# A hybrid DeltaNet and RG-LRU layer: the opening stage reordered, shift and scale of the modulation made as columns, the gate third made in the last scan

## What is computed

```python
xs = x_sample + grid_pos_embed(...)             # sin/cos of 16 grid rows (512 wide) and 64 columns (512 wide)
mod = silu(c) @ ada_w + ada_b                   # once with c_ctx (context), once with c (latent): 3 x 1024
shift, scale, gate = split(mod, 3)
h = rmsnorm(x, pre_w) * (1 + scale) + shift
proj = h @ w_in                                 # q, k, v, z, beta/decay, rg input, rg gate
o_dn = delta_branch(...)                        # 8 heads of 128, both directions, chunks, decays, conv, gated norm
o_rg = rglru_branch(...)                        # width 1024 in 8 blocks, both directions
y = concat([o_dn, o_rg]) @ w_out
return x + gate * rmsnorm(y, post_w), states
```

## Time and profile before

| what | us |
|---|---|
| median of 3 runs | 1523.67 (1518.97 to 1530.37) |
| the profiled execution | 1524.72 |
| its span | 1523.1 |
| PE busy in it | 1391.1 (91%) |
| DVE, ACT, POOL busy | 1027.9, 753.3, 115.3 |

### The profile page before, as it was taken

The page is one execution under the profiler, slowest core; times in us unless marked ns, Lnnn a source line. Parts: engine busy times, 40 slices in busy tenths (PEclk is TensorE's granted clock), DMA queues, the critical chain, the costliest instruction groups (busy, mean ns, idle before and its releaser), DMA issues.

```text
span 1523.1 us, 24595 instructions
## 1 busy us (share of the span) xinstructions
PE 1391.1 (91%) x8182; PEld 1248.2 (82%) x8182; DVE 1027.9 (67%) x2135; ACT 753.3 (49%) x1912; POOL 115.3 (8%) x135
## 2 busy tenths in 40 slices
PE   5966899999999989999999999899989997599997
PEld 1266898899799879988997998799889976388886
DVE  3565477779677877887797778778877966722222
ACT  2351357564646465565647464745666484511111
POOL 0000100010001000100000010001000000212211
PEclk9978999999799999999999999999999998699999
DMA  8702111110111211111111111102111150523440
GB/s 306 249 14 68 28 29 32 57 44 30 40 49 44 57 48 28 60 33 42 44 44 36 53 44 49 55 22 67 33 42 45 44 225 20 153 77 110 124 123 29
DMA packets 95235, 102.79 MB, mean 67 GB/s; under 512 B 4230, under 2 KB 81271, under 8 KB 94089
## 3 DMA queue, kind: packets, MB, share of 16 engines
q1 hardware_dynamic: 92170, 90.70, 19.4%
q0 software_dynamic: 2944, 10.49, 1.8%
HBM read 85.88 MB, written 15.29 MB: 66 GB/s over the span
## 4 chain that ended last, share of the span: by engine, by line
PE 77%; ACT 8%; DVE 6%; issue 5%; DMA 3%; SPq 0%; DVEq 0%; ACTq 0%
PE bank L673 14%; PE bank L675 14%; PE bank L674 14%; PE bank L947 12%; PE bank L901 2%; PE bank L868 2%; PE bank L784 2%; PE bank L909 2%; PE bank L917 2%; PE bank L894 2%; PE bank L889 2%; PE bank L824 2%; DMA arena<-pos_row 2%; PE bank L746 1%; ACT L1089 1%
## 5 line engine op out<-in xcount | busy, mean ns | idle before, releaser
L673 PE MATMUL bank<-hT_hi,w_hi 128*128 128x384 f32 (+1 forms) x1224 | 442.0, 361 | 30.9 <-DVE w_lo L1379 17.6
L675 PE MATMUL bank<-hT_hi,w_lo 128*128 128x384 f32 (+1 forms) x1224 | 419.4, 343 | 0.0
L674 PE MATMUL bank<-hT_lo,w_hi 128*128 128x384 f32 (+1 forms) x1224 | 419.4, 343 | 0.0
L673 PEld LDWEIGHTS bank<-hT_hi,w_hi 128*128 128x128 f32 x1224 | 235.8, 193 | 33.7 <-DVE w_lo L1379 18.5
L674 PEld LDWEIGHTS bank<-hT_lo,w_hi 128*128 128x128 f32 x1224 | 235.9, 193 | 1.2
L675 PEld LDWEIGHTS bank<-hT_hi,w_lo 128*128 128x128 f32 x1224 | 234.9, 192 | 0.0
L1225 ACT ACTIVATE arena<-bank,arena 128x128 f32<-128x128 f32 x272 | 78.7, 369 | 176.2 <-PE bank L901 176.0
L1469 DVE SCALAR_TENSOR_TENSOR arena<-arena 128x1154 f32<-128x1154 f32 x96 | 137.5, 1433 | 3.5 <-DVE arena L1467 1.1
L947 PE MATMUL bank<-wo_hi,ot_hi 128*128 128x512 f32 x288 | 114.3, 397 | 18.8 <-DVE ot_lo L1758 13.5
L947 PE MATMUL bank<-wo_lo,ot_hi 128*128 128x512 f32 x288 | 113.6, 395 | 0.0
L947 PE MATMUL bank<-wo_hi,ot_lo 128*128 128x512 f32 x288 | 113.3, 393 | 0.0
(11 more groups left out here) (224 smaller groups left out, 2388.4 us busy)
## 6 DMA issues: line engine op xcount, KB each, us to landing
w_raw<-w_in SPq DMA_DIRECT2D x51, 512.0 KB, 4.0
arena<-ada_w SPq DMA_DIRECT2D x8, 1536.0 KB, 10.8
arena<-scr_G SPq DMA_DIRECT2D x16, 576.0 KB, 4.8
ot<-scr_o SPq DMA_DIRECT2D x9, 1024.0 KB, 6.7
arena<-x_sample SPq DMA_DIRECT2D x16, 512.0 KB, 7.3
wo<-w_out SPq DMA_DIRECT2D x4, 2048.0 KB, 16.0
scr_o<-arena POOLq DMA_DIRECT2D x8, 576.0 KB, 4.2
arena<-pos_row SPq DMA_DIRECT2D x32, 128.0 KB, 5.5
```

The source lines that it names most:

```text
L673: pe.matmul(out, w_hi[:, slot, k], hT_hi[:, k, cols], start=first, stop=False)
L674: pe.matmul(out, w_hi[:, slot, k], hT_lo[:, k, cols], start=False, stop=False)
L675: return pe.matmul(out, w_lo[:, slot, k], hT_hi[:, k, cols], start=False, stop=last)
```

## The change

- ada_w is loaded in the opening for shift and scale alone (eight slabs of 1 MB). Its product is made as columns: 128 columns of ada_w are the weights, the two columns of silu_c move, 16 products for each of eight k, all in bank 0, which one product with zeros opens. Biases come as columns too. The six row sums and the 16 turns are gone.
- All nine tiles of x have a buffer, and SP issues all loads of the opening without a wait between them. The row half of the position comes from PE (a selection matrix times the 16 rows, into banks 1 and 2), the column half is added by POOL. DVE, ACT and PE work on different tiles in one round i: DVE adds the position row to tile i, makes the mean of i - 1, reciprocal and scale of i - 2, and copies tile i - 3; ACT squares i, takes the root of i - 1 and copies i - 3. The copies to hT are one instruction of 512 columns each.
- Modulation, high and low parts go by column group and k, and PE waits for each k of a group. The order of products is ba(0), k(0), ba(1), ba(2), k(1), transposes, k(2). In DVE's stream the three convolutions move up before and between the sums; ACT's high_w, take_first and Silu are placed anew.
- The gate third: SP loads 4 MB of ada_w, silu_c (by way of DRAM) and the bias before w_out; the last scan waits for them and has 16 products of 512 columns, two in a step; DVE adds the bias after mean_o, SP stores the rows. No wait for gate_stored is left in the opening.
- POOL clears only the border columns of raw.

```diff
-SEGMENTS = [(0, 0, P), (1, P + GAP, 2 * P), (1, P + GAP + 2 * P, 3 * P), (1, P + GAP + 5 * P, 3 * P)]
+SEGMENTS = [[(0, 0, P), (1, P + GAP, 2 * P)], [(1, P + GAP + 2 * P, 3 * P)], [(1, P + GAP + 5 * P, 3 * P)]]
...
-        adaw = early(KT * 3 * D).rearrange("p (k n) -> p k n", k=KT)
-        x_in = early(2 * D).rearrange("p (b n) -> p b n", b=2)
+        adaw = early(KT * 2 * D).rearrange("p (k n) -> p k n", k=KT)
+        x_in = early(NCH * D).rearrange("p (b n) -> p b n", b=NCH)
+        pos_row_in, pos_col_in, row_pick = early(D // 2)[0:16, :], early(D // 2), early(D)[0:16, :]
...
+            for t in range(1, NCH):
+                sp.dma_start(x_in[:, t], x_sample[0, P * (t - 1):P * t, :]).then_inc(x_loaded[t], 16)
+            for k in range(6):
+                load_ada(k)
+            load_w(1, w_in2[:, OFF_B:OFF_B + P].rearrange("(k p) n -> p k n", p=P))
+            load_ada(6)
+            load_ada(7)
+            load_w(0, w_tile("k", 0))
...
+            sp.wait_ge(silu_c_made, 1)
+            sp.dma_start(scr_c, silu_c.rearrange("p s k -> p (s k)")).then_inc(silu_c_stored, 16)
@@ SP, before the w_out loads @@
             sp.wait_ge(projected.sem, projected.prev(h, 18))
+            sp.wait_ge(proj_taken.sem, proj_taken.prev(h, 12))
+            sp.wait_ge(silu_c_stored, 16)
+            sp.dma_start(silu_c_late.rearrange("p s k -> p (s k)"), scr_c).then_inc(gate_in, 16)
+            sp.dma_start(gate_row, ada_b[0:1, 2 * D:].to_broadcast([2, D])).then_inc(gate_in, 16)
+            for q in range(2):
+                sp.dma_start(adaw_gate[:, 4 * q:4 * q + 4, :],
+                             ada_w[0, 512 * q:512 * q + 512, 2 * D:].rearrange("(k p) n -> p k n", p=P)).then_inc(gate_in, 16)
...
+            sp.wait_ge(gate_row_made, 2)
+            sp.dma_start(scr_gate, gate_row).then_inc(gate_stored, 16)
@@ POOL @@
+            gp.wait_ge(pos_in, 48)
+            for n in range(1, NCH):
+                gp.wait_ge(x_loaded[n], 16)
+                gp.tensor_tensor(x_in[:, n, 512:], x_in[:, n, 512:], pos_col_in, ALU.add).then_inc(pos_col_added, 1)
             gp.wait_ge(x_turned, 2 * NCH)
-            gp.memset(raw, 0.0).then_inc(raw_cleared, 1)
             own(gp.memset(sub[0], 0.0))
-            gp.wait_ge(mod_row_made, 6)
-            gp.wait_ge(mod_turned, 1)
-            gp.wait_ge(gate_stored, 16)
             gp.memset(Z, 0.0).then_inc(grounds_made, 1)
+            gp.wait_ge(ada_done, 1)
+            gp.memset(raw[:, :, 0:2], 0.0).then_inc(raw_cleared, 1)
+            gp.memset(raw[:, :, RAW - 1:], 0.0).then_inc(raw_cleared, 1)
@@ PE @@
+            def put_pos_row(n):
+                if n >= 3:
+                    pe.wait_ge(x_added, n - 2)
+                pe.matmul(banks[1 + n % 2][:, :], row_pick[:, P * (n - 1):P * n], pos_row_in, start=True, stop=True)\
+                  .then_inc(pos_row_put, 1)
+            def ada_columns(k):
+                pe.wait_ge(ada_in[k], 16)
+                if k == 0:
+                    pe.matmul(banks[0][:, 0:32], ident, zeros, start=True, stop=False)
+                for m in range(16):
+                    mm = pe.matmul(banks[0][:, 2 * m:2 * m + 2], adaw[:, k, P * m:P * m + P], silu_c[:, :, k],
+                                   start=False, stop=(k == KT - 1 and m == 15))
+                if k == KT - 1:
+                    mm.then_inc(ada_done, 1)
+            put_pos_row(1)
+            for i in range(1, NCH + 2):
+                if i + 1 < NCH:
+                    put_pos_row(i + 1)
+                if i >= 2:
+                    turn_x(i - 2)
+                if i >= 5:
+                    ada_columns(i - 5)
+            for k in range(NCH - 3, KT):
+                ada_columns(k)
...
-            for g, (o, n) in enumerate(GROUPS):
-                pe.wait_ge(h_lo_made, KT * (2 + g) + 1)
-                ...
-            project_first(0)
+            pe.wait_ge(w_lo_made.sem, 1)
+            project_ba(0)
+            pe.wait_ge(w_lo_made.sem, 2)
+            project_k(0)
+            project_ba(1)
+            project_ba(2)
+            project_k(1)
             pe.wait_ge(baT_made, 3)
...
+            project_k(2)
             project_first(1)
@@ PE, last scan: gate_product(k, half) is one matmul 128*2 x 128x512 into bank half @@
                 pe.wait_ge(dZ_taken.sem, dZ_taken.at(b, 30))
+                if last:
+                    pe.wait_ge(gate_in, 16 * 4)
+                    pe.wait_ge(gate_tanh.sem, gate_tanh.at(b, 12))
...
                         fill(1)
+                        if last:
+                            gate_product(step - 1, 0)
...
                     fill(1)
+                    if last and step:
+                        gate_product(step - 1, 1)
...
+            pe.wait_ge(gate_row_made, 2)
             out_tile(0, 0, first=True)
@@ ACT, opening @@
+            for i in range(NCH + 3):
...
+            high_w(1, 16)
+            for g in range(len(GROUPS)):
+                for k in range(KT):
+                    high_h(g, k)
+                    if k + MOD_V < KT:
+                        modulate(g, k + MOD_V)
+                if g == 0:
+                    high_w(0, 16)
-            for n in range(3):
-                take_first(n)
+            take_first(0)
+            take_first(1)
+            high_w(1, 32)
...
-            high_w(1, 32)
-            for n in range(3, 6):
-                take_first(n)
+            take_first(2)
+            take_first(3)
+            high_w(0, 32)
+            take_first(4)
+            take_first(5)
...
-            high_w(0, 32)
-            act.wait_ge(gate_stored, 16)
             act.wait_ge(conv_done.sem, 1)
+            act.activation(kT, RA, ACT.Silu, scale=2.0).then_inc(silued.sem, 1)
             high_w(1, 48)
+            take_first(6)
             act.wait_ge(conv_done.sem, 2)
+            act.activation(qT, RB, ACT.Silu, scale=2.0).then_inc(silued.sem, 1)
+            take_first(7)
+            take_first(8)
+            high_w(0, 48)
@@ DVE @@
+            for i in range(NCH + 3):
...
+            low_w(1, 1)
+            dve.wait_ge(ada_done, 1)
...
+            for g in range(len(GROUPS)):
+                for k in range(MOD_V - 2):
+                    modulate(g, k)
+                for k in range(KT):
+                    low_h(g, k)
+                    if k < 2:
+                        modulate(g, MOD_V - 2 + k)
+                if g == 0:
+                    low_w(0, 2)
...
+            conv_first(0, RA)
+            low_w(0, 4)
             dve.wait_ge(G_summed, 3)
...
+            conv_first(1, RB)
+            low_w(1, 5)
             dve.wait_ge(grounds_made, 1)
             dve.wait_ge(G_stored, 32)
             dve.wait_ge(cols_ready, 1)
+            conv_first(2, xf)
+            low_w(0, 6)
...
             mean_o(HEADS - 1)
+            for half in range(2):
+                dve.wait_ge(gate_done, half + 1)
+                cc = slice(512 * half, 512 * half + 512)
+                dve.tensor_tensor(gate_row[:, cc], gate_row[:, cc], banks[half][0:2, :], ALU.add).then_inc(gate_row_made, 1)
             norm_o(HEADS - 1)
```

More of the change, by code:

```diff
@@ L655, in _ @@
                     mm.then_inc(x_turned, 1)
-                if n < KT:
-                    pe.wait_ge(ada_in[n], 16)
-                    for j in range(6):
-                        mm = pe.matmul(banks[j][0:2, :], silu_c[:, :, n], adaw[:, n, 512 * j:512 * j + 512],
-                                       start=(n == 0), stop=(n == KT - 1))
-                        if n == KT - 1:
-                            mm.then_inc(ada_done, 1)
-            pe.wait_ge(h_made_v, 4 * NCH)
-            for m in range(16):
-                pe.wait_ge(mod_row_made, m // 4 + 1)
-                mm = pe.transpose(banks[6][:, 2 * m:2 * m + 2], mod_row[0:2, P * m:P * m + P], ident[0:2, 0:2])
@@ L1335, in _ @@
                 own(dve.tensor_scalar(to, to, -1.0, None, ALU.mult))
-            def x_tile(buf, n, loaded):
-                prompt = isinstance(n, int) and n == 0
-                dve.wait_ge(x_loaded[buf], loaded)
-                if not prompt:
-                    dve.tensor_tensor(x_in[:, buf], x_in[:, buf], pos[:, buf], ALU.add).then_inc(x_added, 1)
-                dve.wait_ge(x_squared, n + 1)
-                dve.tensor_scalar(x_ss[:, buf:buf + 1], x_ss[:, buf:buf + 1], 1.0 / D, EPS, ALU.mult, ALU.add)\
-                   .then_inc(x_meaned, 1)
-                dve.wait_ge(x_rooted, n + 1)
-                own(dve.reciprocal(x_ss[:, buf:buf + 1], x_ss[:, buf:buf + 1]))
-                dve.tensor_scalar(x_in[:, buf], x_in[:, buf], x_ss[:, buf:buf + 1], None, ALU.mult).then_inc(x_normed, 1)
-                dve.wait_ge(x_turned, 2 * n + 1)
-                first = 0 if prompt else GAP + P * n
-                for k in range(4):
-                    dve.tensor_copy(hT[:, k, bd(first, P)], banks[6][:, P * k:P * k + P]).then_inc(h_made_v, 1)
@@ L1380, in low_w @@
                    .then_inc(w_lo_made.sem, 1)
```

(28 more changed lines are left out.)

270 lines of the change are left out of this document (121 added, 149 removed).

## The result

The changed kernel takes 1571.3 us (median of 4 runs, 1561.1 to 1584.2) against 1523.2 for the kernel before; the ratio is 1.0315 with a 95% interval of 1.0228 to 1.0402. The profiled execution took 1568.78 us with a span of 1567.1, 44.0 more than the span before.

A forecast was written before the change was run, and what follows sets the result against it. PE was taken as the bound, busy 91% of the span. From 1524.7 us, 14.2 less until the modulation, 33.8 less to the first head and 8 more in the last scan gave 1484.7, stated as 1485; range 1468 to 1512.

The forecast's parts named there:

- The head loop is not touched: Head loop: PE nearly dense there and code unedited, so the forecast gave it no term.
- A: Opening until the modulation: it starts at 63 in place of 77.17, 14 us earlier; bounds 49 and 98.
- rival 2: Opening: clock low from start to end, modulation at 98, 35 us more, 1520, no difference; chance 0.08.
- the 0.10 us a pass: Opening's column products on PE: 256 passes at 0.10 us, 3.25 us a k, eight k 26 us.
- rival 3: Opening's column passes, slower case: no overlap with the next weight load, up to 0.34 us a pass, 1546; chance 0.04.
- B: From modulation to first head: turn(kT) 73.5 us after the modulation, 33.8 us less; bounds 36 and 22.
- C: Last scan with the gate's 16 products: 8 us more; bounds 0 and 21.
- the 2.7 us taken off: Last scan: about 1.7 us back where ACT's Silu pair holds PE, about 1 from fewer steps at the lower clock.

The follow-up runs named there:

- run 1: Changed kernel with 72 satisfied waits (36 instructions) more at the start of PE's stream, ahead of the head loop; 1529.87 us, ratio 1.0021.
- run 2: Kernel before with 132 satisfied waits (66 instructions) more, putting its loop where the changed kernel has it; 1563.18 us, ratio 1.0266.
- run 10: Kernel of run 9 with 198 satisfied waits (99 instructions) at the start, putting the loop back at the changed kernel's place; 1529.97 us, ratio 1.0012.
- run 5: Kernel of run 1 with 32 moving columns in the ada products, silu_c's two and 30 of zeros; 1524.43 us, ratio 0.9983.
- Run 6: Changed kernel with shift and scale made as rows again (512 columns of ada_w moving) and one pair of transpose banks; 1498.33 us, ratio 0.9799.
- Run 4: Kernel of run 1 without 12 of the 16 gate products in the last scan; 1528.45 us, ratio 1.0002.
- run 9: Kernel of Run 6 with five idle products of 320 columns in each joins, where PE stands; 1488.04 us, ratio 0.9733.
- run 11: Kernel before with the five idle products in each joins and nothing of the change; 1518.56 us, ratio 0.9927.
- run 3: Kernel before with 60 satisfied waits (30 instructions) more ahead of the loop; 1528.68 us, ratio 1.0009.
- runs 5 to 8: Besides run 5 and Run 6: twenty idle products early in the opening, in the changed kernel (1532.77 us) and Run 6's with 51 wait instructions (1501.97 us).

## Why the prediction was wrong, point by point

The span grew by 44.0 us where 40 less were forecast, an error of 84.

- **"The head loop is not touched", so no term for it: wrong, 43 us.** The instructions are the same, but their place in the stream is not. The new opening has 322 instructions more on PE, which put a block's end some 25 behind the loop's start. Runs 1 and 2 show it in both directions, run 10 once more. The forecast counted what each instruction costs and never the stream's length; the page's instruction queue of before and the waits of PE there (L824 by "issue", 4.1 us in six waits, one at each jump) could have raised the question, but no row of before shows that 66 instructions would be worth 40 us.
- **A, the modulation at 63: wrong, 37 us.** It came at 99.81, where rival 2 had said 98. The term that failed is the 0.10 us a pass: it is 0.207, with the position products at 2.00 and the transposes at 1.90 each, since PE is at the low clock from its first instruction to the first projections. The rival got 0.08. The argument against it was that small unbroken products had brought the clock back in the last scan. Those had 128 moving columns; these have 2, and with 32 (run 5) it is no different. Run 6, which undoes little but the form of the products, has the clock up during the first k and the modulation 28.7 us earlier. The row in which the clock fell about the 2x2 turns was the nearest in kind, and should have had more weight, though PE also idled for 1.2 us ahead of them. That passes and weight loads overlap (against rival 3) was right: a load takes 0.33 us at the low clock, and a pass comes every 0.207. Whether a pass costs 0.10 at the high clock stays open.
- **B, from the modulation to the first head: right.** 75.3 us to turn(kT) for 73.5, and 61.1 from there to the first head for 63.3 before, so 32.4 less for 33.8. The first projection came 2.4 us behind the modulation, as forecast. PE waited 3.1 us for hT_lo where 2.6 were allowed, and for no w_lo.
- **C, the last scan: right.** 10.2 us more for 8: from 53.1 to 63.3 us for the stretch from the first solve to the first output product. Run 4 gives 0.64 us a product for the 0.67 used; the 2.7 us taken off for a hidden ACT pair and for more clock did not come in full.
- **The rest** is small: the scans in the loop 1.1 us less, phase_a 0.9 more, the output tiles 0.5 more. The sum: 22.6 for the later modulation, less 32.4, plus 10.2, 43.1 and 0.3, is 43.8 for a measured 44.0.
- **The side.** The one slower rival had its mechanism in the column passes. None had a place outside the edited code. With the loop's place corrected (run 1) the change is worth nothing, 1.0021: the 10 us won by the first head go to the gate products. Rival 2's 1520 "no difference" would then have been right.

## What to carry to other kernels

When an edit ahead of a loop changes the number of an engine's instructions, look in the profile of after for idle time by "issue" in the loop's first instructions, above all in the middle of a group that has no wait; if it is there, shift the loop by some tens of instructions before you judge the edit. Price small matrix products at both clock levels, and look for what keeps the clock up beside them: here wide moving operands in the opening (28.7 us) and five idle products in PE's standstills (10 us in run 9, 9 us in run 11). The version with both takes 1488 us, 2.7% less than the kernel before, with the rest of the change in it.

## What the runs showed of the hardware

- A jump back costs PE 0.5 to 1.1 us of idle in each pass in all of these kernels. Another 1.0 to 1.8 us follow some 25 instructions on when the loop stands where the changed kernel, run 2 and run 10 have it; 36 or 66 instructions earlier in the stream (run 3 and the kernel before), or 36 later (run 1), nothing does. That this is a block of 16 KB that ends there is the reading that fits all six kernels; the end itself is in no view.
- Such a standstill, far shorter than many that PE has elsewhere, had the low clock with it or within 1 us behind it in three of six heads of the changed kernel (20.5, 20.5 and 37.5 us) and in two of six in run 2, and within some 2 us in three of six in run 10; in the other three of run 10 it cost 1.5 us each and no clock. Which heads lose the clock is not explained. In the changed kernel what it costs is mostly the clock: 1.5 us a head by itself against 7.1 in the mean of the six joins that have it.
- PE's being busy (19.35 of 19.5 us in the row below) did not bring the clock up in the opening: some 54 us of passes with 2 or 32 moving columns stayed at 0.207 and 0.208 each, while passes of 512 columns raised it during the first k. The first record of the clock in the changed kernel is at 107 us; windows before it print 1.00 where the durations say 0.50 (a pass each 0.207 us, projections in steps of 0.32 that turn to 0.18 at 107.4), so durations are what to go by there:

```profile
80.00:99.50 19.50, 19.35 (x91) 19.26 (x91) 1.34 (x3) 0.65 (x1) 2.20 (x4) 1.00 0.00 1
```

- What exactly about the products the clock answers to (moving columns, their total, or the kind of instruction) stays open: runs 5 to 8 exclude only that 32 columns are enough, and that PE's being busy is.
